# One layer of a diffusion backbone on one core: 32 of the 64 later modulation row quarters are summed on VectorE instead of TensorE

## The chip, the cores and the metric

One Trainium2 chip, one core. The time is that of the whole program on the device, in microseconds. The kernel before took 3694.87 us (median of three runs, 3694.04 to 3697.61).

## What is computed

A layer of a hybrid backbone in float32: 512 latent tokens and 256 context tokens of width 2048. A conditioning vector, through silu and `w_mod` (2048 x 12288), gives six rows of modulation (shift, scale and gate of the mixer and of the feed-forward part). The normed and modulated tokens go through one input projection `w_in`; its columns feed a bidirectional mLSTM of four heads and a convolution group (GLU, depthwise convolution of 31 taps, LayerNorm, swish). An output projection and then a product-key expert layer follow. Cut to what the change touches:

```python
mod_x = (silu(c) @ w_mod + b_mod)            # sh1, sc1 | ga1, sh2, sc2, ga2
hx = modulate(rmsnorm(x, g_mix), sh1, sc1)
px = hx @ w_in                               # q, k, v, o, gates | conv columns
u = px_conv[:, :1024] * sigmoid(px_conv[:, 1024:])
y = depthwise_conv(u, 31 taps) + conv_b      # then LayerNorm, silu
x = x + ga1 * (concat(mlstm, conv) @ w_out)
x = x + ga2 * peer(modulate(rmsnorm(x, g_ffn), sh2, sc2))
return rmsnorm(x, g_final)
```

The first 4096 columns of `silu(c) @ w_mod` (sh1, sc1) are needed before the projection. The other 8192, the **later modulation rows**, are needed only at the output projection and behind it. They are 16 blocks of 512 columns, each in four quarters of 512 rows of `w_mod`: 64 row quarters, each 1 MB.

## The kernel before, in words

Weights come from HBM in quarters of 128 x 2048 floats (1 MB) into `ring`, which has four slots. SyncE issues the loads in one order; each waits until TensorE has used what was in the slot (`quarter_used`). A weight quarter r goes through three engines: ScalarE copies it rounded into `w_hi` (`split_hi`, L425; two slots, so quarter r waits until r-2 is used), GpSimd writes the rest into `ring_lo` (`split_lo`, L432, one instruction of 128 x 2048), and TensorE multiplies it as three products (`mm3`, L1753: 48 matmuls of 512 columns for a quarter of the paired stage). A row quarter needs no split: `row_quarter` (L1761) multiplies the slot as it is by `c_rep`, four matmuls of 32 columns of the array each, summed in a PSUM bank.

The stage at issue is the **paired stage**, the loop `for j in range(PAIRED)` on TensorE (L1806): eight blocks j, each of four weight quarters (conv columns for j = 0 to 3, then q and o) and four row quarters in the order W M W M W M M W (`PAIR_W`, `PAIR_M`). ScalarE copies out a block of rows (`copy_row`, L799) and the four banks of a weight block (`empty_set`, L815 to L825). Behind it comes the **key and value stage** (`kv_block(0)` to `(3)`), 16 weight quarters with 96 matmuls each, where no rows are summed. `kv_block(0)` may use banks 4 and 5 when ScalarE has emptied the last block of the paired stage (`set_free`). Row blocks 8 to 15 are summed on TensorE between the attention products (`row_block`).

VectorE does the convolution in the meantime: 8 channel tiles of 31 taps, 248 instructions of 128 x 512 (L1272 for the first tap of a tile, L1276 for the others), each of which reads and writes SBUF alone. Before each group of nine it waits for a split on GpSimd (`conv_turn`):

```python
if n < 198 and n % 9 == 0:
    dve.wait_ge(wsplit_made, 10 + n // 9)
if n >= 198 and (n - 198) % 14 == 0:
    dve.wait_ge(wsplit_made, 32 + (n - 198) // 14)
```

The convolution begins when GpSimd has made the first two GLU products (`glu_done`, L609), behind the split of quarter 9. GpSimd makes four more behind quarter 17, when 62 steps are done, and copies two tiles behind quarter 24, when 124 are (L637). TensorE needs the whole convolution behind `kv_block(0)` (L1873 to L1875).

Of the kernel before, what the change touches and what calls it, by code (L numbers as in the profile page):

```python
# [30 lines left out]
F32R = mybir.dt.float32r  # L31
# [44 lines left out]
MOD1, CONV, QO, KV, MOD2, WO, WQ = 0, 8, 16, 24, 28, 36, 40  # L76
PAIRED = (QO - CONV) // 2 + (KV - QO) // 2
PAIR_W, PAIR_M = (0, 2, 4, 7), (1, 3, 5, 6)


def weight_seq(r):

    if r < 4 * PAIRED:
        return 4 * CONV + 8 * (r // 4) + PAIR_W[r % 4]
    if r < 4 * PAIRED + 16:
        return 4 * KV + r - 4 * PAIRED
    return 4 * WO + r - 4 * PAIRED - 16


def row_seq(b, q):  # L90

    return 4 * CONV + 8 * b + PAIR_M[q] if b < PAIRED else 4 * (MOD2 + b - PAIRED) + q


KV_R, WO_R = 4 * PAIRED, 4 * PAIRED + 16
# [3 lines left out]
def hybrid_layer(nc, x, c, ctx_in, c_ctx, w_mod, b_mod, g_mix, g_ffn, w_in, b_gate, g_mhn, conv_w, conv_b,  # L99
# [11 lines left out]
    with ExitStack() as ctx:  # L111
# [24 lines left out]
        with ExitStack() as mixer:  # L136
# [10 lines left out]
            m_rows = region("m_rows", T, mixer)[0:64, :]  # L147
            g_col = region("g_col", 6 * 64, mixer)[:, :].rearrange("p (s r) -> p s r", r=64)
            e_col = region("e_col", 4 * 64, mixer)[:, :].rearrange("p (s r) -> p s r", r=64)
# [79 lines left out]
        h_sum = top[:, 8216:12312].rearrange("p (j h e) -> p j h e", j=LT, h=HEADS)  # L229
        row_parts = m_rows.rearrange("p (j n) -> p j n", j=4)  # L230

# [75 lines left out]
        q_loaded = [sem(f"q_loaded{h}") for h in range(HEADS)]  # L307
        k_loaded = [sem(f"k_loaded{h}") for h in range(HEADS)]
# [110 lines left out]
        def split_hi(act, r):  # L419

            seq = weight_seq(r)
            act.wait_ge(quarter_full[seq % 4], 16 * (seq // 4 + 1))
            if r >= 2:
                act.wait_ge(quarter_used, weight_seq(r - 2) + 1)
            nc.scalar.activation(weight_slot(r).bitcast(F32R), ring[:, seq % 4, :, :].rearrange("p k n -> p (k n)"),  # L425
                                 ACT.Copy).then_inc(whi_made, 1)

        def split_lo(pool, r):

            at = weight_seq(r) % 4  # L430
# [10 lines left out]
        def _(sp):  # L441
# [6 lines left out]
            def load(seq, src):  # L448

                if seq >= 4:  # L450
                    sp.wait_ge(quarter_used, seq - 3)
                sp.dma_start(ring[:, seq % 4, :, :], src).then_inc(quarter_full[seq % 4], 16)
# [9 lines left out]

            def row_load(b, q):
                load(row_seq(b, q), cols(w_mod, q, 2 * D + b * NB))

            for j, at in enumerate((CONV0, CONV0 + CW, CONV0 + NB, CONV0 + CW + NB, 0, NB, 3 * MW, 3 * MW + NB)):
                for place in range(8):
                    if place in PAIR_W:
                        q = PAIR_W.index(place)
                        load(weight_seq(4 * j + q), cols(w_in, q, at))  # L470
                    else:
                        row_load(j, PAIR_M.index(place))
            for n, at in enumerate((MW, MW + NB, 2 * MW, 2 * MW + NB)):
                for q in range(4):
                    load(weight_seq(KV_R + 4 * n + q), cols(w_in, q, at))

            for q in range(4):
                row_load(8, q)
            sp.wait_ge(quarter_used, 4 * (KV + 4))
            sp.wait_ge(spill_stored, 16 * 8)  # L480
            def qk_load(h):
                sp.dma_start(qT[:, 2 * h:2 * h + 2, :], q_dram[:, 2 * h:2 * h + 2, :]).then_inc(q_loaded[h], 16)
                sp.dma_start(kT[:, 2 * h:2 * h + 2, :], k_dram[:, 2 * h:2 * h + 2, :]).then_inc(k_loaded[h], 16)
# [16 lines left out]
            for b in range(4):  # L500
                for q in range(4):
                    load(weight_seq(WO_R + 4 * b + q), cols(w_out, (q + 2) % 4, b * NB))

            for r in range(U0):
                b, q = r // 4, r % 4
                if b == 0:
                    load(4 * WQ + q, cols(w_query, q, 0))
# [71 lines left out]
        def _(pool):  # L579
# [81 lines left out]
            pool.wait_ge(mrow_stored[0], 16 * 8)  # L661
            pool.wait_ge(mrow_stored[1], 16 * 8)
            pool.wait_ge(m_full, 2 * HEADS)
            pool.dma_start(row_parts, part_dram[:, :].rearrange("j (r n) -> r j n", n=P)).then_inc(parts_loaded, 16)
# [60 lines left out]
        def _(act):  # L725
# [55 lines left out]
            for k in range(KT):  # L781
                act.wait_ge(modulated1, 2 * (k + 1))
                nc.scalar.activation(hT_hi[:, k, :].bitcast(F32R), xT[:, k, :], ACT.Copy).then_inc(h_hi, 1)
                if k == 0:

                    act.wait_ge(quarter_full[0], 16 * (CONV + 1))
# [6 lines left out]

            def copy_row(b, n, buf):

                act.wait_ge(quarter_used, row_seq(b, 3) + 1)
                if b >= 2:
                    act.wait_ge(mrow_stored[b % 2], 16 * (b // 2))
                nc.scalar.activation(buf[:, b % 2, :], bank[:, n, :], ACT.Copy).then_inc(mrow_made, 1)  # L799
                act.wait_ge(mrow_made, b + 1)  # L800
# [102 lines left out]
            for n in range(4):  # L903
                for q in range(4):
                    r = KV_R + 4 * n + q
                    act.wait_ge(quarter_used, weight_seq(r) + 1)
                    if q == 3:
                        empty_kv(n)
                    if r + 2 < WO_R:
                        split_hi(act, r + 2)  # L910
                    if n == 1 and q == 0:
# [3 lines left out]
                    if n == 2 and q == 0:  # L915
                        act.wait_ge(pass_full, 2)
                        act.wait_ge(mrow_stored[0], 16 * 4)
                        act.wait_ge(mrow_stored[1], 16 * 4)
# [71 lines left out]
            for r in range(WO_R, WO_R + 16):  # L990
                act.wait_ge(quarter_used, weight_seq(r) + 1)
# [199 lines left out]
        def _(dve):  # L1191
# [113 lines left out]
            for d in range(2):  # L1305
                r = slice(32 * d, 32 * d + 32)
                g_c, g_x = g_nat[r, 0:C], g_nat[r, C:L]
                m_x, e_x = m_rows[r, :], e_nat[r, :]
                if d:
# [7 lines left out]
            dve.wait_ge(quarter_used, 4 * (KV + 4))  # L1317
# [75 lines left out]
            for f in range(8):  # L1393
                dve.wait_ge(ht_full, f + 1)
                if f == 0:
                    dve.wait_ge(o_loaded, 16)
                    dve.wait_ge(mrow_stored[0], 16 * 8)
                    dve.wait_ge(mrow_stored[1], 16 * 8)
# [6 lines left out]
            dve.wait_ge(parts_loaded, 16)  # L1405
            for j in range(1, 4):
                nc.vector.tensor_tensor(row_parts[:, 0, :], row_parts[:, 0, :], row_parts[:, j, :], ALU.add)\
# [8 lines left out]
            with dve.Fori(0, 2) as i:  # L1416
                for par in range(2):
                    at = bass.ds(i * (2 * NB) + par * NB, NB)
                    dve.wait_ge(quarter_used, i * 8 + 4 * (WO + par + 1))
# [316 lines left out]
        def _(pe):  # L1736
# [54 lines left out]
            def row_unit(b, q, n):  # L1791

                seq = row_seq(b, q)
                pe.wait_ge(quarter_full[seq % 4], 16 * (seq // 4 + 1))
                row_quarter(n, seq % 4, q)

            def weight_parts(r, kk, at):

                cols = slice(kk * NB + at.start, kk * NB + at.stop)
                return [weight_slot(r)[:, cols], ring_lo[:, weight_seq(r) % 4, cols]]  # L1800
# [4 lines left out]

# [333 lines left out]
```

## Time and profile before

| | before |
|---|---|
| median of the runs | 3694.87 us |
| profiled execution, whole time | 3693.22 us |
| its span in the trace | 3691.2 us |
| TensorE busy | 3508.3 us (95%) |
| VectorE busy | 2088.9 us (57%) |
| GpSimd busy | 1987.5 us (54%) |
| ScalarE busy | 1104.4 us (30%) |
| paired stage | about 123 to 537 us |
| key and value stage | about 537 to 834 us |

The span is that of the recorded instructions. Busy shares are means over stages with different limits; the rows of the section below are read from the paired stage. Times in the trace count from the start of the span.

### The profile page before, as it was taken

The numbers are of one execution on the slowest core, as the hardware profiler recorded it, in microseconds if no ns is written. First come the engines' busy times: TensorE is split into PE (matmuls) and PEld (weight loads), VectorE is DVE, ScalarE is ACT, GpSimd is POOL, SyncE is SP. The second block draws the span as 40 slices with busy tenths as digits, with TensorE's granted clock in tenths as the row PEclk, the third lists the DMA queues.
The fourth block names the chain that finished last, engine by engine and source line by source line (L and its number), as shares of the span: only waits on it lengthen the run. The fifth ranks groups of instructions, "written<-read, shape, count | busy, mean of one in ns | idle before, by whom it ended". The sixth has DMA issues, their size and how long they took to land.

```text
span 3691.2 us, 46132 instructions
## 1 busy us (share of the span) xinstructions
PE 3508.3 (95%) x17646; PEld 3001.0 (81%) x17646; DVE 2088.9 (57%) x3619; ACT 1104.4 (30%) x1240; POOL 1987.5 (54%) x942
## 2 busy tenths in 40 slices
PE   5799999998889799999999999999999999999996
PEld 2477778874578589999999999999888888888885
DVE  1317561102521365995477777772566776667669
ACT  3221211123322223232344333443232232232222
POOL 0244432211333545677655565556677777777773
PEclk8799999999999899999999999999999999999998
DMA  9545552228632323777666777668898888888883
GB/s 344 208 162 181 186 179 75 79 71 296 249 125 93 124 90 134 250 295 276 250 259 262 292 283 282 258 261 342 319 338 315 311 311 309 317 321 313 305 308 111
DMA packets 291479, 874.83 MB, mean 237 GB/s; under 512 B 17361, under 2 KB 78081, under 8 KB 237216
## 3 DMA queue, kind: packets, MB, share of 16 engines
q1 hardware_dynamic: 226224, 519.08, 40.0%
q0 software_dynamic: 38704, 281.20, 18.7%
q10 hardware_dynamic: 26432, 73.02, 5.2%
q8 instruction: 68, 1.11, 0.1%
q14 instruction: 51, 0.42, 0.0%
HBM read 803.82 MB, written 69.37 MB: 237 GB/s over the span
## 4 chain that ended last, share of the span: by engine, by line
PE 83%; DVE 6%; DMA 5%; ACT 2%; POOL 2%; issue 1%; ACTq 1%; SPq 0%; DVEq 0%
PE bank L1753 76%; PE bank L2032 2%; PE bank L1946 2%; DMA neurons<-tiny 2%; PE bank L1761 2%; DMA ring<-in_w_mod 2%; DMA ring<-in_w_in 1%; PE bank L1925 1%; POOL ring_lo L432 1%; DVE low L1343 1%; DVE acc L1642 1%; ACT w_hi L425 0%; PE bank L2015 0%; DVE b L1531 0%; ACTq L734 0%
## 5 line engine op out<-in xcount | busy, mean ns | idle before, releaser
L692 POOL TENSOR_TENSOR split<-ring,split 128x1024 fp32r<-128x1024 f32 x544 | 1305.6, 2412 | 689.7 <-ACT split L1012 688.8
L1753 PE MATMUL bank<-h_hi,split 128*128 128x384 f32 (+1 forms) x4608 | 1221.0, 342 | 5.2 <-POOL split L692 3.7
L1753 PE MATMUL bank<-split,a_split 128*128 128x512 f32 x4608 | 1052.1, 390 | 17.1 <-DVE acc L1635 8.8
L1012 ACT ACTIVATE split<-ring 128x1024 fp32r<-128x1024 f32 x544 | 577.2, 1062 | 1595.0 <-PE bank L1753 1566.0
L1753 PEld LDWEIGHTS bank<-split,a_split 128*128 128x128 f32 x4608 | 867.4, 188 | 201.7 <-DVE acc L1635 6.2
L1753 PEld LDWEIGHTS bank<-h_hi,split 128*128 128x128 f32 x4608 | 838.0, 188 | 26.3 <-POOL split L692 4.6
L1753 PE MATMUL bank<-h_lo,split 128*128 128x384 f32 (+1 forms) x2304 | 784.0, 340 | 0.0
L432 POOL TENSOR_TENSOR ring_lo<-ring,w_hi 128x2048 fp32r<-128x2048 f32 x47 | 230.4, 4903 | 432.4 <-ACT w_hi L425 427.6
L1753 PEld LDWEIGHTS bank<-h_lo,split 128*128 128x128 f32 x2304 | 433.0, 188 | 9.9
L1635 DVE TENSOR_TENSOR acc<-acc,bank 128x512 f32<-128x512 f32 x360 | 244.4, 682 | 299.8 <-PE bank L1753 281.2
L1753 PE MATMUL bank<-hT_hi,w_hi 128*128 128x512 f32 (+1 forms) x768 | 292.0, 380 | 23.3 <-POOL ring_lo L432 18.5
L1753 PE MATMUL bank<-hT_lo,w_hi 128*128 128x512 f32 (+1 forms) x768 | 288.6, 376 | 0.0
L1753 PE MATMUL bank<-hT_hi,ring_lo 128*128 128x512 f32 (+1 forms) x768 | 287.7, 375 | 0.0
L1591 DVE TENSOR_SCALAR onehot<-bank,expT,tiny 128x128 fp32r<-128x128 f32 x768 | 276.4, 401 | 0.0
L1276 DVE SCALAR_TENSOR_TENSOR top<-top,conv_col 128x512 f32<-128x512 f32 x240 | 200.3, 908 | 114.2 <-POOL ring_lo L432 114.2
L425 ACT ACTIVATE w_hi<-ring 128x2048 fp32r<-128x2048 f32 x47 | 90.1, 1916 | 433.2 <-PE bank L1753 230.4
L1753 PEld LDWEIGHTS bank<-hT_hi,w_hi 128*128 128x128 f32 x768 | 146.1, 190 | 71.0 <-POOL ring_lo L432 25.5
L1588 DVE TENSOR_SCALAR onehot<-bank,expT 128x128 fp32r<-128x128 f32 x384 | 131.3, 342 | 67.5 <-PE bank L2032 67.5
L1753 PEld LDWEIGHTS bank<-hT_hi,ring_lo 128*128 128x128 f32 x768 | 145.8, 190 | 26.8
L1753 PEld LDWEIGHTS bank<-hT_lo,w_hi 128*128 128x128 f32 x768 | 146.2, 190 | 24.9 <-issue 0.2
L1470 DVE CUSTOM_DVE_ANT_0 rows_b<-bank,rows_b 128x2048 f32<-128x2048 f32 x43 | 98.3, 2285 | 92.3 <-DMA rows_b<-in_u_rows,small 92.1
L1470 DVE CUSTOM_DVE_ANT_0 rows_a<-bank,rows_a 128x2048 f32<-128x2048 f32 x43 | 98.3, 2286 | 76.5 <-DMA rows_a<-in_u_rows,small 76.2
(266 smaller groups left out, 3606.2 us busy)
## 6 DMA issues: line engine op xcount, KB each, us to landing
ring<-in_u_emb SPq DMA_DIRECT2D x128, 1024.0 KB
ring<-in_v_emb SPq DMA_DIRECT2D x128, 1024.0 KB
ring<-in_w_mod SPq DMA_DIRECT2D x96, 1024.0 KB
ring<-in_w_in SPq DMA_DIRECT2D x48, 1024.0 KB
neurons<-tiny ACTq DMA_DIRECT2D x128, 192.0 KB
gate_table<-b ACTq DMA_DIRECT2D x6, 4096.0 KB, 14.7
weigh<-neurons SPq DMA_DIRECT2D x32, 768.0 KB
weigh<-gate_table SPq DMA_DIRECT2D x32, 768.0 KB
```

Source lines behind the costliest of these rows:

```text
L425: nc.scalar.activation(weight_slot(r).bitcast(F32R), ring[:, seq % 4, :, :].rearrange("p k n -> p (k n)"), ACT.Copy).then_inc(whi_made, 1)
L432: nc.gpsimd.tensor_tensor(ring_lo[:, at, :].bitcast(F32R), ring[:, at, :, :].rearrange("p k n -> p (k n)"), weight_slot(r), op=ALU.subtrac ...
L692: nc.gpsimd.tensor_tensor(split[:, r % 2, 1, at].bitcast(F32R), ring[:, r % 4, :, :].rearrange("p k n -> p (k n)")[:, at], split[:, r % 2, ...
L1012: nc.scalar.activation(split[:, q % 2, 0, at].bitcast(F32R), ring[:, q, :, :].rearrange("p k n -> p (k n)")[:, at], ACT.Copy)\
L1276: nc.vector.scalar_tensor_tensor(y, u, w, y, ALU.mult, ALU.add).then_inc(conv_step, 1)
L1470: nc.vector.tensor_tensor_reduce(out=rows, in0=sparse_bank, in1=rows, scale=1.0, scalar=0.0, op0=ALU.mult, op1=ALU.add, accum_out=nval[:, ...
L1588: nc.vector.tensor_scalar(onehot[:, grp % 2, s, 0, :].bitcast(F32R), iota_bank, expT[:, 0, tok], None, ALU.is_equal)
L1591: last = nc.vector.tensor_scalar(onehot[:, grp % 2, s, 1 + part, :].bitcast(F32R), iota_bank, expT[:, 1, tok], gates[:, tok], ALU.is_equal ...
L1635: nc.vector.tensor_tensor(part, part, src, ALU.add).then_inc(sum_free, 1)
L1753: last = mm(out_, left[a].bitcast(F32R), right[b].bitcast(F32R), start=start and n == 0, stop=stop and n == 2)
L1761: last = mm(bank[32 * j:32 * j + 32, n, :], c_rep[:, q * QT + j, :], ring[:, at, j, :], start=q == 0, stop=q == 3, tile_position=(0, 32 * j))
L1946: last = mm(bank[:, 4 + n % 2, 0:HD + 1], probT[:, d, s, j * P:(j + 1) * P], v_aug[:, s, h, :], start=i == 0, stop=i == len(keys) - 1)
```

## The change

Row blocks 0 to 7 (32 row quarters) leave TensorE. VectorE sums them in SBUF: `sum_rows(r)` multiplies the four 128 x 512 pieces of row quarter r by a column of `c_silu` and adds them to one of four accumulators, one instruction each, each waiting for the one before. Quarters 0 to 7 are summed before the convolution starts, 8 to 29 one before each group of eight steps, 30 and 31 before the next two groups of 14. After every four blocks `mean_rows` on TensorE sums the accumulators over the partitions (four matmuls, behind weight quarters 16 and 32), and `store_rows` on ScalarE copies and stores the result.

The ring is dealt out anew until the end of the key and value stage: weights turn through slots 0 to 2, rows have slot 3 and are loaded as two halves of 0.5 MB, each when VectorE has used that half. SyncE issues rows and weights in one order, `row_halves(r)` ahead of `in_load(r + 2)` for r above 4. The rest of the diff follows from this: counts of semaphores, shared places for the accumulators, and loading the stored rows in two transfers.

```diff
+PAIRED, KV_R, WO_R = 8, 32, 48
+MOD1, MOD2, WO, WQ = 0, 24, 32, 36
+
+
+def ring_place(r):
+
+    if r < WO_R:
+        return r % 3, MOD1 + 8 + r // 3
+    return (r - WO_R) % 4, WO + (r - WO_R) // 4
+
+
+def weights_used(r):
+
+    return 32 + r + 1 if r < WO_R else 32 + WO_R + 32 + r - WO_R + 1
+
+
+def rows_used_up(b, q):
+    return 32 + WO_R + 4 * (b - PAIRED) + q + 1
...
+            def weight_load(r, src):
+                if r < 3:
+                    sp.wait_ge(quarter_used, 28 + r + 1)
+                elif r < WO_R:
+                    sp.wait_ge(quarter_used, weights_used(r - 3))
+                elif r < WO_R + 4:
+                    sp.wait_ge(quarter_used, rows_used_up(15, r - WO_R))
+                else:
+                    sp.wait_ge(quarter_used, weights_used(r - 4))
+                load(ring_place(r)[0], src)
...
+            def row_halves(r):
+
+                b, q = r // 4, r % 4
+                for h in range(2):
+                    if r == 0:
+                        sp.wait_ge(quarter_used, 32)
+                    else:
+                        sp.wait_ge(row_added, 4 * (r - 1) + 2 * (h + 1))
+                    sp.dma_start(ring[:, 3, 2 * h:2 * h + 2, :],
+                                 w_mod[0, (4 * q + 2 * h) * P:(4 * q + 2 * h + 2) * P,
+                                       2 * D + b * NB:2 * D + (b + 1) * NB].rearrange("(k p) n -> p k n", p=P))\
+                      .then_inc(row_full[h], 16)
+
+            for r in range(3):
+                in_load(r)
+            row_halves(0)
+            for r in range(1, 4 * PAIRED):
+                if r > 4:
+                    row_halves(r)
+                in_load(r + 2)
+                if r <= 4:
+                    row_halves(r)
+            for r in range(4 * PAIRED + 2, WO_R):
+                in_load(r)
...
             def row_load(b, q):
-                load(row_seq(b, q), cols(w_mod, q, 2 * D + b * NB))
...
+                if b > PAIRED:
+                    sp.wait_ge(quarter_used, rows_used_up(b - 1, q))
+                elif q < 3:
+                    sp.wait_ge(quarter_used, weights_used(WO_R - 3 + q))
+                else:
+                    sp.wait_ge(row_added, 16 * PAIRED)
+                load(q, cols(w_mod, q, 2 * D + b * NB))
+
+            sp.sem_inc(quarter_full[3], 16 * (MOD2 - 8))
...
+            def store_rows(g):
+
+                act.wait_ge(row_meaned, g + 1)
+                nc.scalar.activation(row_place, bank[:, 6, :], ACT.Copy, scale=float(CW)).then_inc(mrow_made, 1)
+                act.wait_ge(mrow_made, g + 1)
+                act.dma_start(part_dram[0, 4 * g * NB:4 * (g + 1) * NB].rearrange("(b n) -> b n", b=4),
+                              row_place[0:P:32, :]).then_inc(mrow_stored[g], 16)
+
...
             for j in range(PAIRED):
                 for q in range(4):
                     r = 4 * j + q
+                    act.wait_ge(quarter_used, weights_used(r))
+                    split_hi(act, r + 2)
+                    if r == 16:
+                        store_rows(0)
                     if q == 3:
-                        copy_row(j, 4 - 4 * (j % 2), row_buf_b)
-                        split_hi(act, r + 1)
-                        act.wait_ge(quarter_used, weight_seq(r) + 1)
-                        split_hi(act, r + 2)
                         empty_set(j)
-                    elif q < 2:
-                        act.wait_ge(quarter_used, weight_seq(r) + 1)
-                        split_hi(act, r + 2)
 
             def empty_kv(n):
...
+            def sum_rows(r):
+
+
+                b, q = r // 4, r % 4
+                rows = row_acc[b % 4]
+                if b == 4 and q == 0:
+                    dve.wait_ge(row_meaned, 1)
+                    dve.wait_ge(mrow_stored[0], 16)
+                for kk in range(QT):
+                    if kk % 2 == 0:
+                        dve.wait_ge(row_full[kk // 2], 16 * (r + 1))
+                    factor = c_silu[:, q * QT + kk:q * QT + kk + 1]
+                    if q == 0 and kk == 0:
+                        nc.vector.tensor_scalar(rows, ring[:, 3, kk, :], factor, None, ALU.mult).then_inc(row_added, 1)
+                        continue
+                    dve.wait_ge(row_added, 4 * r + kk)
+                    nc.vector.scalar_tensor_tensor(rows, ring[:, 3, kk, :], factor, rows, ALU.mult, ALU.add)\
+                        .then_inc(row_added, 1)
+
             def conv_turn(n):
 
-                if n < 198 and n % 9 == 0:
-                    dve.wait_ge(wsplit_made, 10 + n // 9)
-                if n >= 198 and (n - 198) % 14 == 0:
-                    dve.wait_ge(wsplit_made, 32 + (n - 198) // 14)
-
+                if n < 176 and n % 8 == 0:
+                    sum_rows(8 + n // 8)
+                    dve.wait_ge(wsplit_made, 10 + n // 8)
+                if n >= 176 and (n - 176) % 14 == 0:
+                    if n < 176 + 28:
+                        sum_rows(30 + (n - 176) // 14)
+                    dve.wait_ge(wsplit_made, 32 + (n - 176) // 14)
+
+            for r in range(8):
+                sum_rows(r)
             for pair in range(CTILES // 2):
                 dve.wait_ge(glu_done, pair + 1)
                 for tap in range(TAPS):
...
+            def mean_rows(g):
+
+                pe.wait_ge(row_added, 64 * (g + 1))
+                for b in range(4):
+                    last = mm(bank[32 * b:32 * b + 32, 6, :], mean_w[:, 0:32], row_acc[b], start=True, stop=True,
+                              tile_position=(0, 32 * b))
+                last.then_inc(row_meaned, 1)
 
...
                     last.then_inc(quarter_used, 1)
+                    if r == 16:
+                        pe.wait_ge(set_free, j + 2)
+                        mean_rows(0)
 
...
+                    if r == KV_R:
+                        mean_rows(1)
```

## Rows read from the trace of the kernel before

**Rows 1.** Busy time in stretches: us, PE, PEld, DVE, ACT, POOL, PEclk, DMA share, GB/s.

```profile
153.00:164.00 11.00, 0.87 (x9) 0.36 (x2) 5.16 (x9) 6.24 (x5) 4.92 (x2) 0.61 0.55 191
...
530.00:540.00 10.00, 7.08 (x29) 5.38 (x28) 5.56 (x4) 3.68 (x2) 10.00 (x2) 0.89 0.55 194
240.00:510.00 270.00, 265.37 (x1235) 201.25 (x1235) 164.82 (x193) 56.63 (x34) 122.79 (x32) 1.00 0.52 180
```

**Rows 2.** Chain that ended last, in order of time: start, us, what.

```profile
163.64 13.74 PE bank L1753 x48
177.39 1.85 PE bank L1761 x16
179.24 11.15 PE bank L1753 x48
190.39 0.04 issue
190.43 11.17 PE bank L1753 x48
...
495.51 1.00 PE bank L1761 x8
496.51 11.11 PE bank L1753 x48
507.62 1.04 PE bank L1761 x8
508.68 6.76 DMA ring<-in_w_in
...
533.42 1.91 ACT w_hi L425
535.33 1.78 ACT top L825
537.10 0.04 issue
537.15 22.92 PE bank L1753 x121
```

**Rows 3.** The DVE in order of time: start, us, line, count, idle time before.

```profile
248.61 3.09 DVE L1272 TENSOR_SCALAR top<-top,conv_col,chan_col 128x512 f32<-128x512 f32 x2 [90.41 <-POOLq L622]
```

**Rows 4.** The DVE in the convolution, in order of time.

```profile
337.11 5.38 DVE L1276 SCALAR_TENSOR_TENSOR top<-top,conv_col 128x512 f32<-128x512 f32 x8
346.98 20.47 DVE L1276 SCALAR_TENSOR_TENSOR top<-top,conv_col 128x512 f32<-128x512 f32 x18 [4.49 <-POOL ring_lo L432]
375.69 6.06 DVE L1276 SCALAR_TENSOR_TENSOR top<-top,conv_col 128x512 f32<-128x512 f32 x9 [8.23 <-POOL ring_lo L432]
386.24 16.38 DVE L1276 SCALAR_TENSOR_TENSOR top<-top,conv_col 128x512 f32<-128x512 f32 x18 [4.50 <-POOL ring_lo L432]
```

**Rows 5.** GpSimd in order of time, same columns.

```profile
339.84 7.10 POOL L432 TENSOR_TENSOR ring_lo<-ring,w_hi 128x2048 fp32r<-128x2048 f32 x1 [4.78 <-DVE top L1276]
346.91 6.37 POOL L609 TENSOR_TENSOR top<-top 128x512 f32<-128x512 f32 x4
...
379.95 6.26 POOL L432 TENSOR_TENSOR ring_lo<-ring,w_hi 128x2048 fp32r<-128x2048 f32 x1 [4.30 <-ACT w_hi L425]
389.04 5.08 POOL L432 TENSOR_TENSOR ring_lo<-ring,w_hi 128x2048 fp32r<-128x2048 f32 x1 [2.83 <-ACT w_hi L425]
...
434.98 1.64 POOL L637 COPY top<-top 128x512 f32<-128x512 f32 x2
```

**Rows 6.** One line, L1276: ns min/median/max of one instruction.

```profile
L1276 DVE SCALAR_TENSOR_TENSOR top<-top,conv_col x240: 733/743/5103, 251.6 to 568.0; 128x512 f32<-128x512 f32 x120
```

**Rows 7.** One line, L1390: the same columns.

```profile
L1390 DVE TENSOR_TENSOR mix_lo<-top,mix_hi x8: 676/678/692, 1021.7 to 1030.1; 128x512 fp32r<-128x512 f32 x8
```

**Rows 8.** One line, L1272: the same columns.

```profile
L1272 DVE TENSOR_SCALAR top<-top,conv_col,chan_col x8: 533/538/1674, 248.6 to 498.5; 128x512 f32<-128x512 f32 x8
```

**Rows 9.** The DVE, three instructions each waiting for the one before.

```profile
888.89 0.16 DVE L1359 TENSOR_TENSOR den<-bank,den 128x1 f32<-128x1 f32 x1
889.08 0.16 DVE L1362 RECIPROCAL den<-den 128x1 f32<-128x1 f32 x1
889.28 0.48 DVE L1367 TENSOR_SCALAR top<-bank,den 128x256 f32<-128x256 f32 x1
```

**Rows 10.** ScalarE in order of time.

```profile
239.42 1.92 ACT L425 ACTIVATE w_hi<-ring 128x2048 fp32r<-128x2048 f32 x1 [6.31 <-PE bank L1753]
...
319.96 1.92 ACT L425 ACTIVATE w_hi<-ring 128x2048 fp32r<-128x2048 f32 x1 [13.73 <-DMA ring<-in_w_in]
```

**Rows 11.** The transfer queue of SyncE in order of time.

```profile
312.14 11.45 SPq L452 DMA_DIRECT2D ring<-in_w_in  x2
```

**Rows 12.** The DVE waiting for the convolution's mean.

```profile
612.36 4.87 DVE L1279 TENSOR_TENSOR top<-top,bank 128x512 f32<-128x512 f32 x8 [43.59 <-PE bank L1875]
```

More of the change, by code:

```diff
@@ L306, in hybrid_layer @@
         gate_turned = sem("gate_turned")
-        q_loaded = [sem(f"q_loaded{h}") for h in range(HEADS)]
-        k_loaded = [sem(f"k_loaded{h}") for h in range(HEADS)]
+        qk_loaded = [sem(f"qk_loaded{h}") for h in range(HEADS)]
+        row_full = [sem(f"row_full{h}") for h in range(2)]
+        row_added = sem("row_added")
+        row_meaned = sem("row_meaned")
         v_loaded = [sem(f"v_loaded{h}") for h in range(HEADS)]
@@ L419, in split_hi @@
         def split_hi(act, r):
[L421 to L422 removed]
+            at, loads = ring_place(r)
+            act.wait_ge(quarter_full[at], 16 * (loads + 1))
             if r >= 2:
[L424 to L425 removed]
+                act.wait_ge(quarter_used, weights_used(r - 2))
+            nc.scalar.activation(weight_slot(r).bitcast(F32R), ring[:, at, :, :].rearrange("p k n -> p (k n)"),
                                  ACT.Copy).then_inc(whi_made, 1)
         def split_lo(pool, r):
[L430 removed]
+            at = ring_place(r)[0]
             pool.wait_ge(whi_made, r + 1)
@@ L446, in cols, with load @@
                 return rows(w, q)[:, bass.ds(at, NB)].rearrange("(k p) n -> p k n", p=P)
[L448 to L452, printed above, removed]
+            def load(at, src):
+                sp.dma_start(ring[:, at, :, :], src).then_inc(quarter_full[at], 16)
+            def weight_load(r, src):
[8 more added lines that the diff above has]
+                load(ring_place(r)[0], src)
             for q in range(4):
@@ L460, in _ @@
                     sp.dma_start(ring[:, q, :, :], cols(w_mod, q, b * NB)).then_inc(quarter_full[q], 16)
-            def row_load(b, q):
-                load(row_seq(b, q), cols(w_mod, q, 2 * D + b * NB))
[L466 to L472, printed above, removed]
@@ L473, in _, with in_load @@
-            for n, at in enumerate((MW, MW + NB, 2 * MW, 2 * MW + NB)):
-                for q in range(4):
-                    load(weight_seq(KV_R + 4 * n + q), cols(w_in, q, at))
+            AT = (CONV0, CONV0 + CW, CONV0 + NB, CONV0 + CW + NB, 0, NB, 3 * MW, 3 * MW + NB,
+                  MW, MW + NB, 2 * MW, 2 * MW + NB)
+            def in_load(r):
+                weight_load(r, cols(w_in, r % 4, AT[r // 4]))
+            def row_halves(r):
[9 more added lines that the diff above has]
+                      .then_inc(row_full[h], 16)
@@ L501, in _ @@
                 for q in range(4):
-                    load(weight_seq(WO_R + 4 * b + q), cols(w_out, (q + 2) % 4, b * NB))
+                    weight_load(WO_R + 4 * b + q, cols(w_out, (q + 2) % 4, b * NB))
             for r in range(U0):
@@ L506, in _ @@
                 if b == 0:
-                    load(4 * WQ + q, cols(w_query, q, 0))
+                    sp.wait_ge(quarter_used, weights_used(WO_R + 12 + q))
+                    load(q, cols(w_query, q, 0))
                 else:
@@ L910, in _ @@
                         split_hi(act, r + 2)
+                    if n == 0 and q == 1:
+                        store_rows(1)
                     if n == 1 and q == 0:
@@ L1308, in _ @@
                 m_x, e_x = m_rows[r, :], e_nat[r, :]
+                if d == 0:
+                    dve.wait_ge(mrow_stored[0], 16)
+                    dve.wait_ge(mrow_stored[1], 16)
                 if d:
@@ L1403, in _ @@
             mixed_rest(7)
-            dve.wait_ge(parts_loaded, 16)
+            dve.wait_ge(parts_loaded, 32)
             for j in range(1, 4):
-                nc.vector.tensor_tensor(row_parts[:, 0, :], row_parts[:, 0, :], row_parts[:, j, :], ALU.add)\
+                nc.vector.tensor_tensor(row_parts[32:64, 0, :], row_parts[32:64, 0, :], row_parts[32:64, j, :], ALU.add)\
                     .then_inc(rows_summed, 1)
@@ L1808, in _ @@
                 pe.wait_ge(set_free, j + 1)
-                if j:
-                    pe.wait_ge(mrow_made, j)
-                for place in range(8):
-                    if place in PAIR_M:
-                        pe.wait_ge(set_free, j + 2)
-                        row_unit(j, PAIR_M.index(place), 4 - 4 * par)
-                        continue
-                    q = PAIR_W.index(place)
+                for q in range(4):
                     r = 4 * j + q
@@ L1829, in _ @@
                         for m in range(4):
+                            if k == 0 and j == 5 and m == 2:
+                                pe.wait_ge(mrow_made, 1)
                             last = mm3(bank[:, 4 * par + m, :], weight_parts(r, kk, slice(m * P, (m + 1) * P)),
@@ L1907, in row_block @@
             def row_block(b):
[L1908 removed]
+                if b >= 10:
+                    pe.wait_ge(mrow_made, b - 7)
                 for q in range(4):
```

75 lines of the change are left out of this document (32 added, 43 removed).

## The prediction

> **What bounds the kernel now.** I read the busy time in stretches first. From 240 to 510 us, the steady part of the paired stage, TensorE is busy 265.37 of 270 us at full clock, VectorE 164.82, GpSimd 122.79, ScalarE 56.63 [rows 1]: the stage goes by TensorE. The chain of work in order of time gives the pieces. A weight quarter is 11.11 us (48 matmuls), a row quarter 1.00 to 1.04 us [rows 2]. The transfer, the rounding and the split that the chain names between them run beside other weight quarters; TensorE hardly waits for them. A block is 4 x 11.11 + 4 x 1.02 = 48.5 us. So in this stage a row quarter taken off TensorE is worth its full 1.02 us, as long as no other engine is later. Next come the views of VectorE and GpSimd, because the work goes there.
>
> **Two facts of these views decide.** VectorE makes nine convolution steps in 6.05 us, eight in 5.38: 0.665 us a step, while one instruction lasts 0.743 us (two channels alternate, so each step overlaps the next a little) [rows 4, 6]. But 18 steps that should take 12.0 us took 16.38 with one split inside, 4.4 more; one instruction of the line lasted 5.103 us [rows 4, 6]. The other way round, the split begun at 379.95 lasted 6.26 us: VectorE ended its nine steps at 381.75, and the split ended 4.46 us after that [rows 4, 5]. The split begun at 339.84 ended at 346.94, also 4.45 us after VectorE's eight steps (342.49) [rows 4, 5]. So a split and a VectorE instruction that reads and writes SBUF don't run at once: whichever comes second stands. **Their times add.** Now, nine steps and a split are 6.05 + 4.46 = 10.5 us in a turn of 12.2 us, and VectorE has 1.7 us left.
>
> [...]
>
> **What leaves TensorE.** 32 row quarters x 1.02 = 32.6 us, if TensorE sets the end. `mean_rows` puts back two groups of four small matmuls, priced as a row quarter, 1.0 us each. `copy_row` goes from ScalarE and `store_rows` comes; ScalarE is busy a fifth of the stage, so nothing.
>
> **What VectorE gets.** Four instructions a row quarter, each waiting for the one before. The trace has no such instruction. Nearest is the convolution's, of the same operation and size, 0.743 us [rows 6]; a chained one starts 0.03 us behind its predecessor's end [rows 9]. Below is the sum of two tiles without a factor, 0.678 us [rows 7]. I take 0.776. The first of a block is a TENSOR_SCALAR, 0.54 [rows 8]. A row quarter is then 4 x 0.776 less 0.06 on average, 3.05 us. (The Trainium skill, VectorE: DVE Perf Modes, on the fixed latency of SBUF sources, has a row of 58 cycles plus the 512 elements at 0.96 GHz, 0.594 us; by it my sum below would be 92 x 0.15 = 14 us shorter. It says itself that the row is too low, and the trace has 0.743.)
>
> A turn now is eight steps 5.38, a row quarter 3.05, a wait 0.1 and a split 4.46: **13.0 us against TensorE's 11.11**. VectorE falls behind, by some 2 us a turn.
>
> **Who waits for VectorE.** SyncE's queue is in order: `in_load(r + 2)` stands behind `row_halves(r)`, whose halves wait until VectorE has summed row quarter r - 1. A late VectorE thus holds back the weights. At first there is slack: a weight quarter's slot is free when quarter r - 3 is used, 22 us before it is wanted, and load, rounding and split are 7.3 + 1.9 + 4.5. It is used up within about five turns; from there TensorE has VectorE's pace. The six GLU products behind the start, the two copies, and ScalarE's and VectorE's wait for `store_rows(0)` lie inside this.
>
> **The start.** Up to quarter 2 nothing changes: it begins at 163.64 and ends at 177.39, because ScalarE is through the tokens only then [rows 2]. VectorE is idle for 90.41 us before its first step at 248.61 [rows 3]; row quarters 0 to 7 fit there. Without the rows quarters 3 to 7 end at 177.4 + 5 x 11.11 = 232.9, where now it is 239.3 (ScalarE is released then [rows 10]). The first step comes 248.6 - 239.3 = 9.3 us behind that end, so VectorE begins row quarter 8 at 242.2.
>
> **The sum**, up to the end of row quarter 30, which comes behind 176 steps:
>
> - 23 row quarters (8 to 30) x 3.05 = 70.2
> - 176 steps x 0.665 = 117.0; 23 turns x 0.1 = 2.3
> - 23 splits (10 to 32) x 4.46 = 102.6
> - products and copies: 18 steps with four products and a split took 20.47, that is 8.5 above 12.0 and 4.0 above the split [rows 4, 5]; so 4.0, another 2.0 for the two products at the start, 1.6 for the copies [rows 5]: 7.6
>
> 242.2 + 70.2 + 119.3 + 102.6 + 7.6 = 541.9 us. Then row quarter 31's second half is issued and, behind it, weight quarter 33. The load takes 7.3 us (now 6.76 by the chain, 7.8 from issue at 312.14 to use at 319.96 [rows 2, 10, 11]). ScalarE rounds it, 1.91, and only then empties the last block, 1.78, on which `kv_block(0)` waits [rows 2]. With 0.3 for the hand-overs that is 553.2, where the trace has 537.15 [rows 2]: **+16.0 us**.
>
> To it comes `mean_rows(1)`, 1.0. TensorE stands some ten us before this stage; after such a gap (0.87 busy in 11 us, granted clock 0.61) a quarter took 13.74 instead of 11.15 [rows 1, 2], 2.6 more. Today's gap of 3.8 us at 533 leaves the clock at 0.89 [rows 1] and costs about 1, so 1.5 more. Shorter gaps in the stage hide behind VectorE. **Sum: +18.5.** The remaining 58 convolution steps, the last row quarter and some four splits are 58 x 0.665 + 3.1 + 4 x 4.5 = 60 us behind 542, about 615 with the waits for splits; `kv_block(0)` ends at 553 + 68 = 621, so the mean still finds the convolution done. Now it has 43.59 us in hand [rows 12], then some 6. Behind it the kernel is the same but for a second small transfer, beside other work: nothing. 3693.2 + 18.5 = 3711.7 for the profiled execution; the median stands 1.65 above that one: **3713.4**.
>
> Bounds: row instructions of 0.678 give -9, 22 splits instead of 23 -4.5, a split of 4.33 -3: 3697. Loads of 9 us, and gaps at a lower clock that don't hide, give +16: 3729.
>
> **Rivals.**
> First, **TensorE stays the bound**: the row instructions, or the splits, run beside each other after all, or GpSimd gets in so seldom that it costs nothing. Then quarter 31 ends at 232.9 + 24 x 11.11 + 1.0 = 500.5, the next stage begins 3.8 later at 504.3, 32.8 before today's, and with `mean_rows(1)` it is -31.8: 3663. It decides where steps, row quarter and split take 11.11 or less together, two us below what the rows add up to. For it: no row instruction is in the trace. Against: the steps are of the same kind, and the lock shows in each turn. 0.14.
> Second, **a tie**: row instructions near 0.68 and half of the products overlapped, about 3697, or a little more saved. 0.16.
> Third, **late row halves**: the second half of a row quarter is issued when the one before it is summed, and wanted 5.38 + 1.55 = 6.9 us later where no split lies between; a 1 MB load takes 7.3. If both halves take as long, a turn is up to 0.8 longer, 23 turns 18: 3732. 0.12.
> That the rows don't leave TensorE can't be: their matmuls are gone from the loop.
> The forecast itself, 3704 to 3726, has 0.58.
>
> **Range and chances.** 0.2% is 7.4 us, about what a measurement of this kernel tells from none. Faster by more: the first rival and a little, 0.14. Within: the tie, 0.15. Slower: 0.71. The range leaves out the first rival and a part of the third: 3690 to 3732.
>
> **What would show it.** Right: VectorE nearly without idle time from 242 to 560 us; weight quarters on TensorE 11.1 us each with gaps of 2 to 4 us every one or two, released by splits; loads of `w_in` issued behind the rows' instructions; the next stage starting near 553. Wrong: row instructions under 0.7 us or splits of 4.6 with VectorE busy beside them; a stage start near 504 means the first rival; VectorE idle for transfers of `w_mod`, the third. A convolution that ends later than `kv_block(0)` would add to the loss.

## The result, and the profile after

The changed kernel takes 3703.98 us (median of 16 runs, 3698.47 to 3709.73). The kernel before took 3696.91 (16 runs, 3691.19 to 3701.38) beside it. The ratio is 1.0023, interval 1.0016 to 1.0030: **slower by 0.23%, 6 to 11 us**. The prediction was 3713.4, slower, with a range of 3690 to 3732. Direction and range held, and the bound moved as forecast; the loss by the medians, 7.1 us, is about four tenths of the 18.5 that the forecast had.

The profiled execution of the changed kernel took 3708.57 us, with a span of 3706.8. It is 15.4 us above the profiled execution of the kernel before, while the medians differ by 7.1; where the rest stands is said behind the account of the prediction.

| | before | after |
|---|---|---|
| TensorE busy | 3508.3 us | 3491.9 us |
| VectorE busy | 2088.9 us | 2267.9 us |
| key and value stage begins | 537.15 us | 539.85 us |
| `kv_block(0)` ends | 605.46 us | 610.22 us |
| first scores begin (L1925, after: L2010) | 849.00 us | 857.02 us |

First the busy time of the same stretch as in [rows 1], with the same columns, of the changed kernel:

```profile
240.00:510.00 270.00, 247.97 (x1044) 200.28 (x1043) 263.05 (x250) 50.12 (x28) 113.17 (x31) 0.96 0.54 175
```

VectorE is busy 263 of 270 us, TensorE 248; before it was 165 and 265. Time for which a split holds a VectorE instruction up counts as busy here, so a part of the 263 is waiting. The bound has changed hands, although GpSimd does no more than before.

The chain of the changed kernel, in order of time, from the last row quarter of the paired stage on, answers to [rows 2]:

```profile
164.07 57.38 PE bank L1831 x240
...
526.40 0.76 DVE gate_cols L1321
527.60 8.45 DMA ring<-in_w_in
536.12 1.91 ACT w_hi L432
538.03 1.78 ACT top L879
539.85 18.79 PE bank L1831 x93
558.64 1.00 PE bank L1887 x8
559.63 50.59 PE bank L1831 x288
610.22 6.87 PE bank L1960 x16
...
838.47 3.05 ACT top L907 x6
841.55 9.12 DMA v<-top
...
851.12 5.86 DMA low<-k
```

A load of `w_in` starts when VectorE has ended a row quarter (527.16), and `kv_block(0)` waits for what follows: the path that the prediction named. The third part, around 841, it did not have: the store of the last values takes 9.12 us, and the queries and keys wait for it.

VectorE of the changed kernel in order of time, L1321 a row instruction and L1351 a convolution step; it answers to [rows 3, 4]:

```profile
241.64 0.48 DVE L1318 TENSOR_SCALAR top<-ring,c_silu 128x512 f32<-128x512 f32 x1 [21.17 <-POOLq L665]
...
300.51 5.39 DVE L1351 SCALAR_TENSOR_TENSOR top<-top,conv_col 128x512 f32<-128x512 f32 x8
305.82 3.18 DVE L1321 SCALAR_TENSOR_TENSOR gate_cols<-ring,c_silu,gate_cols 128x512 f32<-128x512 f32 x4
308.91 9.72 DVE L1351 SCALAR_TENSOR_TENSOR top<-top,conv_col 128x512 f32<-128x512 f32 x8
318.56 7.51 DVE L1321 SCALAR_TENSOR_TENSOR gate_cols<-ring,c_silu,gate_cols 128x512 f32<-128x512 f32 x4
```

Eight steps are 5.39 us alone and 9.72 with a split inside; a row quarter is 3.18 alone and 7.51 with one. There is no gap between the groups, and behind 242 us VectorE never waits for a transfer of `w_mod`: the third rival, late row halves, didn't come.

### The profile page after: what moved, and what is told of

The parts are those of the page before. It is cut to its first block, busy times and chain, and to the rows that moved or that the text cites. A ratio compares the mean times of both kernels' runs of the same rounds, so it can differ in the third digit from the quotient of the medians.

```text
span 3706.8 us, 45821 instructions
## 1 busy us (share of the span) xinstructions
PE 3491.9 (94%) x17406; PEld 3005.9 (81%) x17406; DVE 2267.9 (61%) x3747; ACT 1100.2 (30%) x1234; POOL 1987.4 (54%) x943
## 4 chain that ended last, share of the span: by engine, by line
PE 76%; DVE 14%; DMA 4%; issue 2%; ACT 2%; POOL 1%; ACTq 0%; SPq 0%; DVEq 0%; POOLq 0%
PE bank L1831 69%; DVE top L1351 4%; PE bank L2117 2%; DMA ring<-in_w_mod 2%; DMA neurons<-tiny 2%; PE bank L2031 2%; DVE top L1321 1%; PE bank L2010 1%; PE bank L1839 1%; DVE gate_cols L1321 1%; DVE low L1421 1%; DVE low L1298 1%; DVE m_rows L1321 0%; DVE acc L1720 0%; DMA ring<-in_w_in 0%
## 5 line engine op out<-in xcount | busy, mean ns | idle before, releaser
L1831 PE MATMUL bank<-split,a_split 128*128 128x512 f32 x4608 | 1055.3, 391 | 18.5 <-DVE acc L1713 9.8
L1351 DVE SCALAR_TENSOR_TENSOR top<-top,conv_col 128x512 f32<-128x512 f32 x240 | 217.9, 980 | 15.3 <-POOL ring_lo L439 15.3
## 6 DMA issues: line engine op xcount, KB each, us to landing
gate_table<-b ACTq DMA_DIRECT2D x6, 4096.0 KB, 14.7
```

Of the source, the lines that this page charges most:

```text
L1351: nc.vector.scalar_tensor_tensor(y, u, w, y, ALU.mult, ALU.add).then_inc(conv_step, 1)
L1831: last = mm(out_, left[a].bitcast(F32R), right[b].bitcast(F32R), start=start and n == 0, stop=stop and n == 2)
```

## The experiments

The theory: **VectorE's and GpSimd's times add; their sum is longer than TensorE's weight quarter; and SyncE's queue, with row loads ahead of weight loads, passes VectorE's delay on to TensorE.** The rivals: TensorE itself is slower in its new order (clock, `mean_rows`, three slots); VectorE alone is too slow, whatever GpSimd does; the 9.12 us of the store are chance.

### VectorE's part taken away

```diff
                     dve.wait_ge(row_added, 4 * r + kk)
+                    if r >= 8:
+                        dve.sem_inc(row_added, 1)
+                        continue
                     nc.vector.scalar_tensor_tensor(rows, ring[:, 3, kk, :], factor, rows, ALU.mult, ALU.add)\
```

> The changed kernel without the SCALAR_TENSOR_TENSOR instructions of row quarters 8 to 31 (only counted as done; transfers, waits, the first instruction of each block and everything else stay): the later rows of modulation are wrong. Theory (VectorE's time added to GpSimd's sets the pace): eight steps and a split are 9.6 us, under the 11.1 of a weight quarter, so TensorE sets the pace again; the next stage begins at 504 to 512, 28 to 36 us earlier than in the changed kernel, and the program takes about 3672 (ratio 0.993). Rival (TensorE loses its time through its clock, mean_rows or the three slots for weights): the next stage begins at 530 or later and the program stays above 3690.

Measured: 3661.83 us, ratio 0.9907 (0.9891 to 0.9922). Its chain in order of time:

```profile
494.03 1.91 ACT w_hi L432
...
497.76 18.99 PE bank L1834 x93
516.74 0.99 PE bank L1890 x8
517.74 50.59 PE bank L1834 x288
568.33 6.87 PE bank L1963 x16
```

The stage begins at 497.76, 42 us earlier than in the changed kernel and 39.4 earlier than before. From 240 to 480 us TensorE is busy all the time, at full clock:

```profile
240.00:480.00 240.00, 240.00 (x1063) 197.75 (x1062) 138.01 (x184) 51.55 (x28) 119.64 (x31) 1.00 0.61 210
```

The three slots and the clock thus cost nothing to speak of, and `mean_rows` its 1 us each time; the rival that TensorE itself is slower falls. It also prices what left TensorE: the stage begins 39.4 us before that of the kernel before, where I had 32.8. Most of the difference stands in ScalarE's order of time in this kernel: it is released by TensorE every 10.88 us, not 11.11.

```profile
483.15 1.92 ACT L432 ACTIVATE w_hi<-ring 128x2048 fp32r<-128x2048 f32 x1 [8.96 <-PE bank L1834]
494.03 1.91 ACT L432 ACTIVATE w_hi<-ring 128x2048 fp32r<-128x2048 f32 x1 [8.96 <-PE bank L1834]
```

A weight quarter is 10.88 us when no row quarter stands beside it. So a row quarter between weights cost about 1.02 + 0.23 = 1.25 us, and 32 of them some 40: an estimate from these rows, which leaves out that of two weight quarters in a row the second was cheaper already before, and the small waits of both kernels.

### GpSimd's part halved, VectorE untouched

```diff
-            nc.gpsimd.tensor_tensor(ring_lo[:, at, :].bitcast(F32R), ring[:, at, :, :].rearrange("p k n -> p (k n)"),
-                                    weight_slot(r), op=ALU.subtract).then_inc(wsplit_made, 1)
+            part = slice(0, 1024 if 10 <= r <= 33 else 2048)
+            if 10 <= r <= 33:
+                nc.gpsimd.memset(ring_lo[:, at, 1024:2048], 0.0)
+            nc.gpsimd.tensor_tensor(ring_lo[:, at, part].bitcast(F32R),
+                                    ring[:, at, :, :].rearrange("p k n -> p (k n)")[:, part],
+                                    weight_slot(r)[:, part], op=ALU.subtract).then_inc(wsplit_made, 1)
```

> The changed kernel with GpSimd's split halved for weight quarters 10 to 33: it subtracts 1024 of the 2048 columns and fills the other half with zeros (so the small parts of half of these weights are left out); VectorE's instructions are all there. Theory (GpSimd's time adds to VectorE's): each split holds VectorE up for about 2.2 us instead of 4.25, plus what the fill takes if that counts too; eight steps, a row quarter and a split are then 10.6 us, under the 11.1 of a weight quarter. The next stage begins at 495 to 510 instead of 540 and the program takes about 3670 (ratio 0.993); if the fill holds VectorE up as well, 3675 to 3685. Rival (VectorE alone is too slow, or the four chained instructions a quarter are): VectorE's instructions are untouched, the next stage begins at 535 to 540, 3704.

Measured: 3662.32 us, ratio 0.9908 (0.9893 to 0.9923). The order of time of VectorE, then of GpSimd, in that kernel:

```profile
264.80 7.52 DVE L1355 SCALAR_TENSOR_TENSOR top<-top,conv_col 128x512 f32<-128x512 f32 x8
272.25 3.17 DVE L1325 SCALAR_TENSOR_TENSOR top<-ring,c_silu,top 128x512 f32<-128x512 f32 x4
275.33 7.53 DVE L1355 SCALAR_TENSOR_TENSOR top<-top,conv_col 128x512 f32<-128x512 f32 x8
```

```profile
264.99 0.96 POOL L441 MEMSET ring_lo<- 128x1024 f32 x1 [7.06 <-ACT w_hi L432]
265.91 2.55 POOL L442 TENSOR_TENSOR ring_lo<-ring,w_hi 128x1024 fp32r<-128x1024 f32 x1
275.88 0.96 POOL L441 MEMSET ring_lo<- 128x1024 f32 x1 [7.42 <-ACT w_hi L432]
276.79 2.86 POOL L442 TENSOR_TENSOR ring_lo<-ring,w_hi 128x1024 fp32r<-128x1024 f32 x1
```

VectorE does exactly the work of the changed kernel, and the loss is gone: the next stage begins at 496.45. "VectorE alone is too slow" falls. A turn is now 7.45 + 3.08 = 10.53 us, just under the 10.88 of TensorE. The half split holds eight steps up by 7.52 - 5.39 = 2.1 us; the fill of 0.96 us beside the same steps adds nothing to that. The Trainium skill (SBUF — State Buffer, "Who interferes with whom") says that a VectorE instruction with two SBUF inputs contends with a GpSimd instruction that reads SBUF and not with one that only writes it; these rows agree.

### The queue of SyncE

```diff
             for r in range(1, 4 * PAIRED):
-                if r > 4:
-                    row_halves(r)
                 in_load(r + 2)
-                if r <= 4:
-                    row_halves(r)
+                row_halves(r)
```

> The changed kernel with in_load(r + 2) ahead of row_halves(r) for every r, so that no weight load waits for VectorE's sums. Theory (the queue of SyncE ties the weights to VectorE): TensorE keeps 11.1 us a quarter until GpSimd waits for 62 and 124 convolution steps; VectorE's own pace stays (12.7 to 13 us for eight steps, a row quarter and a split), so row quarter 31 and the convolution end at nearly the same time as in the changed kernel (547 and about 590 against 601). The next stage begins near 530 instead of 540, kv_block(0) ends near 600 instead of 610: 8 to 10 us faster than the changed kernel, about 3695, level with the kernel before. Rival (VectorE and GpSimd alone hold the stage, the queue doesn't matter): the next stage still begins at 538 to 540, no gain.

Measured: 3696.01 us, ratio 0.9998 (0.9989 to 1.0008). ScalarE in order of time:

```profile
528.52 1.91 ACT L432 ACTIVATE w_hi<-ring 128x2048 fp32r<-128x2048 f32 x1 [12.44 <-DMA ring<-in_w_in]
```

The stage begins at 532.2, 7.6 us earlier, and `kv_block(0)` ends at 603.32 instead of 610.22. But the edit doesn't do all that its expectation says: weight loads still wait for VectorE's sums. `in_load(r + 2)` now stands behind `row_halves(r - 1)`, whose halves wait for the sum of row quarter r - 2; it has moved up by one row quarter. The chain shows it, with the end of row quarter 29 at 521.77 in front of the load that the changed kernel issued behind the end of row quarter 30 (527.16):

```profile
516.79 4.98 DVE gate_cols L1318
...
522.21 6.24 DMA ring<-in_w_in
```

In between TensorE runs ahead and waits elsewhere for the same thing, for instance 8.5 us in front of the first `mean_rows`, for row quarter 15 (TensorE in order of time):

```profile
337.12 1.03 PE L1884 MATMUL bank<-m_rows,mean_w 128*32 128x512 f32 x1 [8.53 <-DVE gate_cols L1318]
```

So the queue is one of the ways by which VectorE's delay reaches TensorE, and one place in it is worth 7 to 9 us (7.6 at the stage, 8.0 between the medians, 9 between the ratios). With this alone, the kernel is level with the one before. What a queue without this tie would give at this spreading, no run shows.

### The store of the last values

```diff
-            for q in range(4):
+            for q in (3, 0, 1, 2):
                 row_load(8, q)
```

> The changed kernel, with row quarter (8, 3) issued ahead of (8, 0) to (8, 2). Its slot has been free since the last sum on VectorE, but in the changed kernel it stands in SyncE's queue behind (8, 2), which waits for the last weight quarter, and both loads of 1 MB then run beside the store of the last values (landing 9.1 us after issue, where the kernel before has 5.8). Theory: the store lands 3 us earlier, so the queries and keys too, and the program is 3 us faster than the changed one (about 3701, ratio to the kernel before 1.0015). Rival: the store was slow by chance in that execution; landing stays at 8 to 9 us and nothing is gained. Nothing moves ahead of 834 us in either case.

Measured: 3699.45 us, ratio 1.0012 (1.0003 to 1.0021). Up to 838 us all is as in the changed kernel (`kv_block(0)` ends at 610.14); then its chain has:

```profile
841.46 5.83 DMA v<-top
...
847.74 5.78 DMA low<-k
```

The store lands in 5.83 us instead of 9.12, and from there on this execution is 3.2 us ahead of the changed kernel's (the output projection begins at 1037.08 instead of 1040.28). The medians differ by 4.5, the two ratios by 0.0011, 4 us; their intervals overlap, so it is the landing in the trace, and not the time, that shows this clearly. The changed kernel issues two loads of 1 MB at the end of the last weight quarter:

```profile
838.47 0.92 SPq L456 DMA_DIRECT2D ring<-in_w_mod  x2
```

and the kernel before only one (its queue, same view):

```profile
833.70 0.37 SPq L452 DMA_DIRECT2D ring<-in_w_mod  x1
```

The second of the two has its slot free since 547 us. It stands in the queue behind one whose slot is free only now. Every version that kept this order (the changed kernel, weights first, no sums, half split) shows a landing of 9.1 to 9.5 us, and every one without it (the kernel before, this one and the two below) one of 5.8 to 5.9; the chance falls.

### Two other spreadings of the same sums

The time of VectorE and GpSimd together counts only up to the end of the convolution. So rows should go where these two have time. The first attempt put 12 row quarters in front of the convolution instead of 8, and the other 20 between its steps; both changes of the queue are in it, and the second `mean_rows` comes three weight quarters later:

```diff
+                if n < 72 and n % 18 == 0:
+                    sum_rows(12 + n // 18)
+                if 72 <= n < 248 and (n - 72) % 11 == 0:
+                    sum_rows(16 + (n - 72) // 11)
...
-            for r in range(8):
+            for r in range(12):
                 sum_rows(r)
```

> A version meant to keep what the change gains: row quarters 0 to 11 summed before the convolution, where VectorE waits for 84 us and works for 30; 12 to 15 one for each 18 steps, 16 to 31 one for each 11 steps up to step 237; weight loads ahead of row loads in SyncE's queue; the second mean_rows behind kv_block(0), in bank 7; row quarter (8, 3) loaded first. Theory (only VectorE's time beside GpSimd's counts, up to the end of the convolution): the next stage begins at 504 to 515, the convolution ends near 586 (20 row quarters x 3.1, 248 steps x 0.665, 26 splits x 4.3 behind 242), kv_block(0) near 588: 17 us ahead of the kernel before, about 3680 (ratio 0.9955). Rival: row loads in pairs hold back the weights at the start, or the convolution still ends at 600; then 3690 to 3697.

Measured: 3690.58 us, ratio 0.9990 (0.9981 to 0.9999). The rival's figure, and VectorE's order of time shows why. In the changed kernel row quarter 8 had begun at 241.64, behind 21.17 us of waiting (first row of its order of time above); this version has in the same place

```profile
247.97 1.54 DVE L1321 SCALAR_TENSOR_TENSOR top<-ring,c_silu,top 128x512 f32<-128x512 f32 x2 [0.45 <-DMA ring<-in_w_mod]
...
255.51 0.49 DVE L1318 TENSOR_SCALAR gate_cols<-ring,c_silu 128x512 f32<-128x512 f32 x1 [2.59 <-DMA ring<-in_w_mod]
...
266.62 0.99 DVE L1348 TENSOR_SCALAR top<-top,conv_col,chan_col 128x512 f32<-128x512 f32 x2
```

A row quarter in front costs its load, not its sum: with one slot in two halves, VectorE waits 0.4 to 3.5 us in front of most of them. The 84 us hold some ten of them, not twelve, and the first step came at 266.6 instead of 250.5. That gave back what the shorter turns had saved. The stage began at 521, but the convolution ended only at 598.7, and TensorE, through with `kv_block(0)` 6.2 us earlier, had to wait for it (the waits of TensorE):

```profile
PE bank L1960 <- DVE top L1352: 6.2, 1, 6.2
```

The mean of the convolution began at 598.78, where the changed kernel has 610.22.

The second attempt leaves 8 in front, puts 14 between the steps (each 14, later each 16 steps), two behind them, and eight behind the subtraction of the mean, where VectorE had nothing to do; `mean_rows` moves behind quarters 24 and 39, and both changes of the queue are in it again:

```diff
+                if n < 112 and n % 14 == 0:
+                    sum_rows(8 + n // 14)
+                if 148 <= n < 244 and (n - 148) % 16 == 0:
+                    sum_rows(16 + (n - 148) // 16)
...
+            for r in (22, 23):
+                sum_rows(r)
             dve.wait_ge(pass_full, 1)
...
+            for r in range(24, 32):
+                sum_rows(r)
```

> Another spreading of the same sums: row quarters 0 to 7 before the convolution as in the changed kernel, 8 to 15 one for each 14 steps, 16 to 21 one for each 16 steps from step 148 on, 22 and 23 behind the convolution, 24 to 31 behind the subtraction of the mean, where GpSimd and VectorE have time; mean_rows behind quarters 24 and 39, the second in bank 7; weight loads ahead of row loads; row quarter (8, 3) first. Theory (only VectorE's and GpSimd's time together up to the end of the convolution counts, 14 row quarters instead of 24): 242 + 248 x 0.665 + 14 x 3.1 + 25 splits x 4.25 + 5 = 561, below the 568 at which TensorE ends kv_block(0) when nothing holds it. So the next stage begins at 498 to 506, kv_block(0) ends at 568 to 575, and the program takes 3662 to 3670 (ratio 0.991 to 0.993), faster than both. Rival: the queries of SyncE and GpSimd's waits for 62 and 124 steps hold TensorE, as in the version with 12 quarters ahead; then 3680 to 3690.

Measured: 3664.81 us, ratio 0.9913 (0.9899 to 0.9926), **faster than both, by 32 us than the kernel before**. Its chain:

```profile
507.89 66.77 PE bank L1835 x381
574.65 6.87 PE bank L1963 x16
...
807.17 5.85 DMA v<-top
```

`kv_block(0)` ends at 574.65, 6 us behind the version without sums. The convolution ended at 571.5 (VectorE in order of time), 10 us later than my sum said, and did not hold TensorE:

```profile
570.10 1.42 DVE L1351 SCALAR_TENSOR_TENSOR top<-top,conv_col 128x512 f32<-128x512 f32 x2 [4.50 <-POOL ring_lo L439]
```

How much of the gain is the spreading and how much the queue, no run separates. But the half split, without either change of the queue, was 35 us faster than the kernel before: where VectorE keeps up, the order of the loads costs little more than the 3.3 us of the store.

## Why the prediction was right, and where it was off

**The bound changes hands: right.** Two turns of steps, row quarter and split take 25.48 us in the rows above (300.51 to 325.99), 12.7 each, more than TensorE's quarter; I had 13.0 against 11.11, and the 11.11 should have been 10.88. Both halves of the claim were shown by taking one away at a time.

**VectorE's sum: the mechanism right, 14.7 us too long.** I had the end of row quarter 30 at 541.9; it was 527.16. By terms:

- Start of row quarter 8: 242.2 forecast, 241.64 measured, -0.5.
- 23 row quarters with their waits: 72.5 forecast, 69.5 measured (17 at 3.09, 6 first ones at 2.83), -3.0. One instruction was 0.76 to 0.77 us.
- 176 steps: 117.0 forecast, 116.6 measured.
- The splits are **the mis-sized term**: 23 x 4.46 = 102.6 forecast, 22 x 4.25 = 93.5 measured. One split costs VectorE 4.2 to 4.4 us: 9.72 - 5.39 = 4.33 and 7.51 - 3.18 = 4.33 in the rows above, 7.33 - 3.17 = 4.16 and 9.79 - 5.38 = 4.41 at the ends of the range; 4.25 is about the middle. I had taken 4.46 from the end of a step to the end of a split, GpSimd's side of the lock, though [rows 4] held VectorE's own side, 16.38 against 12.0, which is 4.4. And the 23rd split began only at 529.29, behind row quarter 30:

```profile
511.52 5.05 POOL L439 TENSOR_TENSOR ring_lo<-ring,w_hi 128x2048 fp32r<-128x2048 f32 x1 [4.61 <-ACT w_hi L432]
529.29 4.87 POOL L439 TENSOR_TENSOR ring_lo<-ring,w_hi 128x2048 fp32r<-128x2048 f32 x1 [12.72 <-ACT w_hi L432]
```

- Products, copies and small waits: 7.6 forecast, 5 to 6 left over in the measured time.

**From there to the next stage:** 11.3 forecast, 12.7 measured; the load took 8.45 instead of 7.3. So the stage began at 539.85, 2.7 us late, not 16.0.

**`mean_rows(1)` and the clock:** 2.5 forecast; `kv_block(0)` took 70.37 instead of 68.31, so 2.1. TensorE had waited 9.2 us in two pieces before it, and from 530 to 540 us its granted clock was 0.58, as forecast (some ten us, 0.61). The mean found the convolution done, as forecast: VectorE waited 15.54 us for it (43.59 in [rows 12]), of which 6.87 are the mean itself.

```profile
617.13 4.87 DVE L1354 TENSOR_TENSOR top<-top,bank 128x512 f32<-128x512 f32 x8 [15.54 <-PE bank L1960]
```

**"Behind it the kernel is the same but for a second small transfer": wrong.** That step missed the order of the four loads of row block 8 and cost 3.3 us. I had looked at which slot each waits for, not at what stands in front of it in the queue. Together: 2.7 + 2.1 + 3.3 = 8.1 us by the time of the first scores, where the two medians differ by 7.1 and the ratio says 5.9 to 11.1. So the mechanism that was forecast cost 4.8 us, not 18.5, and that the measured loss comes as near as it does is in part luck: 3.3 us of it have a cause that the prediction put at nothing. With that cause removed (row quarter (8, 3) first) the loss is 1 to 8 us.

**What left TensorE** was worth about 40 us by the estimate above, not 32.6: I had priced the four matmuls and not the 0.23 us that they cost the weight quarter beside them. In the changed kernel this hides behind VectorE. By my own sum for the first rival it would make 3656 out of 3663; the version without sums, which is nearly that rival and has the store's 3.3 us too, measured 3661.83.

**The profiled execution's other 7 us.** It is 15.4 above the one of before. Of this 7.9 stand in front of 1250 us, the loss explained so far, and the rest behind, where the programs are the same. Three us of the rest stand between 1250 and 1795:

```profile
1249.59 65.58 PE bank L1753 x288
...
1559.07 224.92 PE bank L1753 x1296
```

is the kernel before: 309.48 us from row to row. The changed kernel has 1257.49 and 1568.45, 310.96, and then 226.5 instead of 224.92. Most versions show the larger figures, but the one with the half split, whose code behind the mixer is that of the changed kernel, has 309.48 (from 1210.62 to 1520.10) and 224.92 in its chain too.

So the change does not bring them by itself. The last 4.6 us come behind 1795; executions of one kernel differ by 11 us over 16 runs. The cause of both parts stays open, and the medians don't need them: they stand as the rows up to 1250 do, 7.1 and 7.9 us behind the kernel before for the changed kernel, 3.4 and 4.8 behind for (8, 3) first, level and 1.7 ahead for weights first.

## What to carry to other kernels

Two engines that lock each other out are one engine: add their times before moving work to the one that looks idle, and take the price of the lock from the victim's rows. A queue in order passes delay on; for every load ask what stands in front of it, and put the load whose slot is free first. Work that is needed late should go where both engines are idle, and that is worth trying before giving it up: here the same 32 row quarters cost 7 us when 24 of them lie between the convolution steps, and gain 32 when 14 lie there and ten behind it, with the loads in a better order.

## What the runs showed of the hardware

- A GpSimd fill of SBUF (0.96 us for 128 x 1024) beside convolution steps on VectorE did not hold them up; a subtraction that reads SBUF did, for 2.1 us (1024 columns) and 4.2 to 4.4 us (2048 columns).
- Which side of the lock waits is not fixed. GpSimd's split took from 4.6 up to 10.2 us in the version with 12 quarters in front (GpSimd in order of time, of that version):

```profile
320.29 10.22 POOL L439 TENSOR_TENSOR ring_lo<-ring,w_hi 128x2048 fp32r<-128x2048 f32 x1 [6.69 <-ACT w_hi L432]
331.16 4.62 POOL L439 TENSOR_TENSOR ring_lo<-ring,w_hi 128x2048 fp32r<-128x2048 f32 x1 [0.65 <-ACT w_hi L432]
```

  and 17.16 us in the version with weights first, where it was issued into an unbroken stream of 28 steps (VectorE from 546.32 to 564.96) and ended 4.4 us behind the stream:

```profile
552.25 17.16 POOL L439 TENSOR_TENSOR ring_lo<-ring,w_hi 128x2048 fp32r<-128x2048 f32 x1 [17.03 <-ACT w_hi L432]
```

- A weight quarter of 48 matmuls took 10.88 us without float32 row matmuls beside it and 11.11 with them.
- A store of 1.5 MB landed in 5.8 us beside one load of 1 MB and in 9.1 to 9.5 beside two.
